# Gates of A and B, the first merge stage and branch A's merge products computed half of the tokens at a time

## What is computed

```python
def merge_and_residual(x, h, gate, br, a_out, b_out, c_out, lw):
    ya = (a_out.reshape(B, T, A_WIDTH) * jax.nn.silu(br['ga'])) @ lw['w_proj_a']
    yb = (b_out.reshape(B, T, B_WIDTH) * jax.nn.silu(br['gb'])) @ lw['w_proj_b']
    yc = (c_out * jax.nn.silu(br['gc'])) @ lw['w_proj_c']
    g_a, g_b, g_c = jnp.split(jax.nn.sigmoid(h @ lw['w_gate'] + lw['b_gate']), N_BRANCH, axis=-1)
    y = (g_a * ya + g_b * yb + g_c * yc) @ lw['w_out']
    return layer_norm(DEEPNORM_ALPHA * x + gate * y, lw['ln_g'], lw['ln_b'])
```

## Time and profile before

| what | value |
|---|---|
| median of 3 runs | 1398.67 us (1397.64 to 1399.9) |
| the profiled execution | 1399.68 us |
| span in its profile | 1397.9 us |
| PE busy | 1361.0 us, 97% of the span |
| ACT, DVE, POOL busy | 627.7, 769.3, 682.8 us |
| PE's waits for ACT at L987 (gates) | 1.6 us in 4 |
| PE's waits for DVE at L987 (y) | 1.9 us in 4 |
| PE's wait "issue" at L987 | 1.7 us, once |

### The profile page before, as it was taken

How to read it: one execution, slowest core, us unless ns; L and a number is a source line. 1 busy time by engine, 2 the same in 40 slices (tenths; PEclk the granted TensorE clock), 3 DMA queues, 4 the chain that set the end, 5 groups by cost and what they waited for, 6 DMA issues and landing times.

```text
span 1397.9 us, 22509 instructions
## 1 busy us (share of the span) xinstructions
PE 1361.0 (97%) x8654; PEld 1260.6 (90%) x8654; DVE 769.3 (55%) x1618; ACT 627.7 (45%) x1314; POOL 682.8 (49%) x490
## 2 busy tenths in 40 slices
PE   7999999999999999999999999999999999999997
PEld 5898989899899999999888988998989989999986
DVE  5756773163883511656695567732558725037558
ACT  5436876334765211213264468851367733122131
POOL 3455565234565354344654566643246554444450
PEclk9999999999999999999999999999999999999999
DMA  9312001122013254354321210011211041225321
GB/s 378 122 61 80 17 31 46 61 80 76 31 47 115 82 167 154 103 211 137 121 105 56 70 61 31 17 60 62 78 60 46 31 136 61 75 76 196 121 91 75
DMA packets 36761, 126.87 MB, mean 91 GB/s; under 512 B 5040, under 2 KB 5808, under 8 KB 36656
## 3 DMA queue, kind: packets, MB, share of 16 engines
q1 hardware_dynamic: 29952, 108.54, 22.9%
q10 hardware_dynamic: 6704, 16.90, 3.3%
HBM read 119.66 MB, written 5.77 MB: 90 GB/s over the span
## 4 chain that ended last, share of the span: by engine, by line
PE 88%; DVE 4%; POOL 2%; ACT 2%; issue 2%; DVEq 0%; ACTq 0%; POOLq 0%
PE ps L987 42%; PE ps L968 8%; PE ps L919 7%; PE ps L921 7%; PE ps L920 7%; PE ps L1137 4%; PE ps L1127 3%; PE ps L1129 3%; PE ps L1148 2%; PE ps L1149 2%; PE ps L1004 1%; POOL w_lo L1854 1%; POOL p_f_a L1880 1%; PE ps L1156 1%; PE ps L1012 1%
## 5 line engine op out<-in xcount | busy, mean ns | idle before, releaser
L1854 POOL TENSOR_TENSOR w_lo<-raw,w_hi 128x1024 fp32r<-128x1024 f32 x148 | 360.0, 2438 | 270.6 <-ACT w_hi L1192 185.0
L987 PE MATMUL ps<-h_hi,w_hi 128*128 128x320 f32 x992 | 230.0, 313 | 3.3 <-issue 1.7
L987 PE MATMUL ps<-h_hi,w_lo 128*128 128x320 f32 x992 | 227.2, 310 | 0.0
L987 PE MATMUL ps<-h_lo,w_hi 128*128 128x320 f32 x992 | 226.6, 310 | 0.0
L1192 ACT ACTIVATE w_hi<-raw 128x1024 fp32r<-128x1024 f32 x148 | 154.4, 1055 | 148.2 <-DMA raw<-in_weights 66.2
L987 PEld LDWEIGHTS ps<-h_hi,w_hi 128*128 128x128 f32 x992 | 170.0, 189 | 16.1 <-issue 3.9
L987 PEld LDWEIGHTS ps<-h_hi,w_lo 128*128 128x128 f32 x992 | 166.8, 189 | 0.0
L987 PEld LDWEIGHTS ps<-h_lo,w_hi 128*128 128x128 f32 x992 | 166.7, 189 | 0.0
L919 PE MATMUL ps<-w_hi,h_hi 128*128 128x512 f32 (+1 forms) x360 | 129.2, 359 | 1.2 <-POOL w_lo L1854 1.0
L921 PE MATMUL ps<-w_hi,h_lo 128*128 128x512 f32 (+1 forms) x360 | 127.6, 354 | 0.0
L920 PE MATMUL ps<-w_lo,h_hi 128*128 128x512 f32 (+1 forms) x360 | 127.5, 354 | 0.0
(11 more groups left out here) (194 smaller groups left out, 3044.8 us busy)
## 6 DMA issues: line engine op xcount, KB each, us to landing
raw<-in_weights SPq DMA_DIRECT2D x190, 512.0 KB, 3.3
raw_more<-in_weights SPq DMA_DIRECT2D x10, 512.0 KB, 10.4
x<-in_x_sample ACTq DMA_DIRECT2D x6, 512.0 KB, 9.6
x_mid<-x ACTq DMA_DIRECT2D x5, 512.0 KB, 2.6
x<-x_mid ACTq DMA_DIRECT2D x5, 512.0 KB, 7.1
y_sample<-x SPq DMA_DIRECT2D x3, 512.0 KB, 2.6
pack<-in_pack ACTq DMA_DIRECT2D x2, 528.0 KB, 6.5
x<-in_x_sample SPq DMA_DIRECT2D x2, 512.0 KB, 5.1
```

The source lines that it names most:

```text
L987: last = pe.matmul(ps[:, s + half, 0:HALF], w[:, u % RING, cols], acts[:, k, half * HALF:(half + 1) * HALF], start=k == 0 and part == 0, s ...
L1854: did(pool.tensor_tensor(w_lo[:, n % RING, :], raw_tile(r), w_hi[:, n % RING, :], ALU.subtract), w_ready)
```

## The change

Sixteen stages in each layer now go by halves: the four gates of A, the first three gates of B, the first merge stage of branch A (z 0) and the eight y of branch A. Their first halves get events of their own (`g1`, `z1`, `y1`), which `whole` puts in front of the stage's own event. Each half takes a single bank, by the rule for single banks; the stages that were by halves before stay pinned to 6 and 7 (`in_steps`). `half_rows` now also serves a whole stage in one piece: all matmuls of the first half, then all of the second, and PE waits for each bank when its half begins. ACT's Silu and copy and DVE's product are done once a half on 128x320 numbers. POOL's product of attention and gate waits for both halves of the gate; ACT's sigmoid of z 0 waits for both halves of z 0. Loads, splits and the order of all other events are as before.

```diff
--- before.py
+++ after.py
@@ -92,15 +92,20 @@
 
 def by_halves(stage):
 
+    return stage[0] == "gT" or stage[0] == "y" and stage[2] == 0 or stage[0] == "z" and stage[2:] == (0, 0)
+
+
+def in_steps(stage):
+
     return stage[0] == "gT" and (stage[2] in ("c", "u") or stage[2:] == ("b", KT_B - 1))
 
 
 def first_half(stage):
-    return ("g1", *stage[1:])
+    return (stage[0][0] + "1", *stage[1:])
 
 
 def whole(stage):
-    return chunks(stage, 1) + [stage]
+    return chunks(stage, 1) + ([first_half(stage)] if by_halves(stage) else []) + [stage]
 
 
 def attention(l, br, first_filler, filler, last_filler, lag, ahead):
@@ -546,9 +551,9 @@
             take(("out", e[1], 1, e[2]), 1, until=("out", e[1], 1, e[2]))
         elif kind == "cr" and by_halves(e[2]):
             if e[3] == 0:
-                take(first_half(e[2]), 1, 6, until=first_half(e[2]))
-            elif e[3] == GATE_CHUNKS // 2:
-                take(e[2], 1, 7, until=e[2])
+                take(first_half(e[2]), 1, 6 if in_steps(e[2]) else None, until=first_half(e[2]))
+            if e[3] == e[4] // 2:
+                take(e[2], 1, 7 if in_steps(e[2]) else None, until=e[2])
         elif kind == "cr" and e[3] == 0:
             take(e[2], 2, until=e[2])
         elif kind == "mm" and e[3] == 0:
@@ -955,31 +960,34 @@
                     if not ends:
                         did(last, w_used)
 
-                def half_rows(stage, i):
-                    half, u, each = 2 * i // GATE_CHUNKS, USERS[stage], KT_D * 3 // (GATE_CHUNKS // 2)
-                    mine = stage if half else first_half(stage)
-                    s, i = PLACE[mine][0], i % (GATE_CHUNKS // 2)
+                def rows_of(stage):
+                    if stage[0] == "y":
+                        return o_hi, o_lo, KT_B, stage[3] % 2 * KT_B * P
+                    return h_hi, h_lo, KT_D, 0
+
+                def half_rows(stage, i, n):
+                    u = USERS[stage]
                     if i == 0:
-                        begin(mine)
                         pe.wait_ge(w_ready, u + 1)
-                    work = [(k, part) for k in range(KT_D) for part in range(3)]
-                    for k, part in work[each * i:each * (i + 1)]:
-                        w, acts = ((w_hi, h_hi), (w_hi, h_lo), (w_lo, h_hi))[part]
-                        last = pe.matmul(ps[:, s, 0:HALF], w[:, u % RING, k * P:(k + 1) * P],
-                                         acts[:, k, half * HALF:(half + 1) * HALF],
-                                         start=k == 0 and part == 0, stop=k == KT_D - 1 and part == 2)
-                    if i == GATE_CHUNKS // 2 - 1:
-                        did(last, filled[s])
+                    hi, lo, kt, first = rows_of(stage)
+                    work = [(half, k, part) for half in range(2) for k in range(kt) for part in range(3)]
+                    for half, k, part in work[len(work) * i // n:len(work) * (i + 1) // n]:
+                        mine = stage if half else first_half(stage)
+                        s, opens, closes = PLACE[mine][0], (k, part) == (0, 0), (k, part) == (kt - 1, 2)
+                        if opens:
+                            begin(mine)
+                        w, acts = ((w_hi, hi), (w_hi, lo), (w_lo, hi))[part]
+                        last = pe.matmul(ps[:, s, 0:HALF], w[:, u % RING, first + k * P:first + (k + 1) * P],
+                                         acts[:, k, half * HALF:(half + 1) * HALF], start=opens, stop=closes)
+                        if closes:
+                            did(last, filled[s])
 
                 def channel_rows(stage, i, n):
                     s, u = PLACE[stage][0], USERS[stage]
                     if i == 0:
                         begin(stage)
                         pe.wait_ge(w_ready, u + 1)
-                    if stage[0] == "y":
-                        hi, lo, kt, first = o_hi, o_lo, KT_B, stage[3] % 2 * KT_B * P
-                    else:
-                        hi, lo, kt, first = h_hi, h_lo, KT_D, 0
+                    hi, lo, kt, first = rows_of(stage)
                     work = [(k, part, half) for k in range(kt) for part in range(3) for half in range(2)]
                     for k, part, half in work[len(work) * i // n:len(work) * (i + 1) // n]:
                         w, acts = ((w_hi, hi), (w_hi, lo), (w_lo, hi))[part]
@@ -1078,7 +1086,7 @@
                             else:
                                 pe.wait_ge(o_done, O_PER_LAYER * l + (10, 20)[stage[2]])
                         if by_halves(stage):
-                            half_rows(stage, i)
+                            half_rows(stage, i, n)
                         else:
                             channel_rows(stage, i, n)
                     elif kind == "kt":
@@ -1381,8 +1389,8 @@
                         if br == "u":
                             continue
                         s = wait_filled(act, e)
-                        if kind == "g1" or e in TANH_NO:
-                            half = (g_c if br == "c" else g_t)[:, c, HALF * (kind == "gT"):HALF * (1 + (kind == "gT"))]
+                        half = (g_c if br == "c" else g_t)[:, c, HALF * (kind == "gT"):HALF * (1 + (kind == "gT"))]
+                        if in_steps(("gT", *e[1:])):
                             did(act.activation(half, ps[:, s, 0:HALF], ACT.Copy, scale=0.5), drained[s])
                             if kind == "g1":
                                 continue
@@ -1397,8 +1405,10 @@
                             wait_filled(act, ("in", l, "kv_a", T - 1))
                         if br == "b" and c == 0:
                             wait_filled(act, ("y", l, 0, KT_D - 1))
-                        did(act.activation(g_t[:, c, :].rearrange("p (b n) -> p b n", b=2), ps[:, s:s + 2, 0:HALF], ACT.Silu),
-                            drained[s])
+                        did(act.activation(half, ps[:, s, 0:HALF], ACT.Silu), drained[s])
+                    elif kind in ("z1", "z") and e[2:] == (0, 0):
+                        s, first = wait_filled(act, e), HALF * (kind == "z")
+                        did(act.activation(merge[:, 0, first:first + HALF], ps[:, s, 0:HALF], ACT.Copy), drained[s])
                     elif kind == "z":
                         _, l, r, j = e
                         s = wait_filled(act, e)
@@ -1415,6 +1425,8 @@
                                                ACT.Sigmoid, bias=b_gate_col[:, r * KT_D + j:r * KT_D + j + 1]), drained[s])
                     elif kind == "sg":
                         _, l, j = e
+                        if j == 0:
+                            wait_drained(act, ("z1", l, 0, 0))
                         wait_drained(act, ("z", l, 0, j))
                         did(act.activation(merge[:, j, :], merge[:, j, :], ACT.Sigmoid, bias=b_gate_col[:, j:j + 1]), sg_ready)
                     elif kind == "mix":
@@ -1745,15 +1757,17 @@
                             dve.wait_ge(gate_made, TANH_NO[("gT", l, "c", KT_B - 1)] + 1)
                         half = g_c[:, c, HALF * (kind == "gT"):HALF * (1 + (kind == "gT"))]
                         did(dve.tensor_tensor(half, ps[:, s, 0:HALF], half, ALU.mult), drained[s])
+                    elif kind in ("y1", "y") and e[2] == 0:
+                        _, l, _, j = e
+                        s = wait_filled(dve, e)
+                        dve.wait_ge(sg_ready, KT_D * l + j + 1)
+                        half = merge[:, j, HALF * (kind == "y"):HALF * (1 + (kind == "y"))]
+                        did(dve.tensor_tensor(half, ps[:, s, 0:HALF], half, ALU.mult), drained[s])
                     elif kind == "y":
                         _, l, r, j = e
                         s = wait_filled(dve, e)
                         y = ps[:, s:s + 2, 0:HALF]
-                        if r == 0:
-                            dve.wait_ge(sg_ready, KT_D * l + j + 1)
-                            m2 = merge[:, j, :].rearrange("p (b n) -> p b n", b=2)
-                            did(dve.tensor_tensor(m2, y, m2, ALU.mult), drained[s])
-                        else:
+                        if r > 0:
                             wait_drained(dve, ("z", l, r, j))
                             n = 2 * KT_D * l + (r - 1) * KT_D + j
                             if n >= 2:
@@ -1887,6 +1901,7 @@
                         if gate in TANH_NO:
                             pool.wait_ge(gate_made, TANH_NO[gate] + 1)
                         else:
+                            wait_drained(pool, first_half(gate))
                             wait_drained(pool, gate)
                         did(pool.tensor_tensor(og_sum(n), og_sum(n), og_part(g_t, g), ALU.mult), og_ready)
                     elif kind == "ol":
```

## The result

The changed kernel takes 1388.43 us (1388.33 to 1388.55, 4 runs) against 1398.16 (1397.24 to 1399.9, 4 runs) for the one before: ratio 0.9929, 95% interval 0.9912 to 0.9946. That is 9.7 us less, inside the stated range and 0.07 us from the forecast.

The account below looks back on a forecast made before the run. PE bounds the kernel, so its idle time counts. Terms 1.47 + 1.46 + 5.8 + 1.46 = 10.19 us off the profiled 1399.68 gave 1389.5, less 1.01 for the median: 1388.5; range 1385.5 to 1394.0.

Parts of the forecast that it names:

- The eight waits: PE's four waits on gate drains and four on y products, both layers: all vanish, 5.53 us, each y 0.73.
- Layer 1's gates: Layer 1's start of A: two gate waits and the shorter last drain, 0.81 + 0.60 + 0.27 = 1.68 us.
- layer 0's gates: Layer 0's start of A: two gate waits and the shorter last drain, 2 x 0.60 + 0.27 = 1.47 us.
- The start of A in layer 1: Branch A's attention in layer 1: first and second maximum start sooner, 5.8 us, between 1.68 and 6.7.
- the wait at z 1: Layer 1: PE's 1.69 us "issue" was bank 7 holding tile 4's transposed queries; it goes.
- the half clock: Layer 1, 805.9 to 812.6: PE's 0.50 clock behind the idle stretches goes, saving up to 3.35 us.
- layer 0's clock: Layer 0, 119.8 to 123.1: the half-clock stretch stays; if it moved or went, 1.65 us either way.
- A: Rival: only the marked waits go, layer 1's wait or clock fall stays; gain 6.1, 1392.6 us; chance 0.20.
- C: Rival: in 32 stages, separating matmuls with shared weights costs time, about 1472 us; decides from 17.7 ns a pair; chance 0.05.
- B: Rival: new idle at attention starts makes the clock fall elsewhere, price 1.7 to 3.4 us, 1390 to 1392; chance 0.12.
- D: Rival: time doesn't move, same banks or gains lost at next waits; 1395.8 to 1399 us; chance 0.07.
- Gates B at 0: Shorter last drains of gates B and z: counted as 0, bound 0.27 us a layer.

Follow-up runs that it names:

- experiment 3: Kernel before with only the sixteen y of branch A by halves: 1396.63 us, ratio 0.9985.
- experiment 4: Changed kernel with the sixteen y of branch A whole again: 1391.29 us.
- experiment 1: Kernel before with only the eight gates of A by halves; gates of B, z and y whole: 1400.5 us, ratio 1.0015.
- experiment 6: Changed kernel with layer 1's transposed queries of tile 4 put in bank 7: 1391.39 us.
- 5: Kernel before, no halves, with layer 1's transposed queries of tile 4 in bank 0 instead of 7, tile 0's kept in bank 3: 1396.32 us, ratio 0.9983.
- 7: Changed kernel with the still whole stages running all first-half matmuls before the second half's, banks and drains unchanged: 1389.89 us.
- experiment 11: Changed kernel run again unaltered, on the chip of the follow-up runs: 1389.25 us.
- experiment 8: Changed kernel with the first three gates of B whole again: 1389.01 us.
- experiment 2: Kernel before with only gates of A by halves and layer 0's whole z 0 put in banks 1 and 2: 1397.27 us, ratio 0.9987.
- 10: Changed kernel with ACT's load of the exp table moved between the two drains of z 0 in both layers: 1387.05 us.

## Why the prediction was right, and where it was not

**The eight waits** went in full. The y were worth 2.98 by the leads of experiment 3 and 2.0 to 2.9 by the times of experiment 4, against 2.92. Layer 1's gates gave 1.81 with their shorter drain in experiment 1, against 1.68; layer 0's gates 1.52 against 1.47: the kernel after came to gate 1 0.31 us later (its transposes at 66.70 against 66.39, out of a start that the change doesn't touch) and led by 1.21 (110.84 - 109.63) when the keys' work began behind the last gate.

**The start of A in layer 1** gave 5.84, against 5.8. Its parts were not known singly, and the runs give them: 1.81 for the gates (experiment 1), 1.38 for the wait at z 1 (experiment 6), 2.75 for the half clock (experiment 3; its bound was 3.35). Together that is 5.94, close to the whole, though each part comes from another kernel. That the "issue" was a bank is shown from both sides (5 and 6).

**The step that failed** is layer 0's clock, "the keys' waits before it aren't touched", so the stretch "stays". The waits stayed and the stretch was gone: 1.4 us, from a lead of 1.21 to 2.63. PE's two waits for keys, before and after:

```profile
115.13 0.41 PE L1096 MATMUL ps<-ident_r,k_st 128*128 128x128 f32 x2 [1.08 <-DVE k_st L1521]
118.36 0.30 PE L1127 MATMUL ps<-k_hi,q_t 128*128 128x128 f32 x1 [1.40 <-DVE k_lo L1661]
```

```profile
113.92 0.41 PE L1104 MATMUL ps<-ident_r,k_st 128*128 128x128 f32 x2 [0.81 <-DVE k_st L1533]
117.15 0.30 PE L1135 MATMUL ps<-k_hi,q_t 128*128 128x128 f32 x1 [1.39 <-DVE k_lo L1673]
```

The first is 0.27 us shorter, as much as the last gate's drain; no run shows whether that decides. It is hardly chance alone: the stretch is there in all three profiles with whole gates of A (before, experiments 3 and 5), and in none of the nine profiles with halved gates besides experiment 1, whose half clock comes earlier, behind its 4.06 us. Why the clock stays up there with the halves is open. The range had it as 1.65 either way.

The other slip is the 1.01 us by which the profiled execution stood above the median: I took it off the forecast as if the changed kernel had it too. It does not: 1388.39 and 1388.43. The two errors, 1.1 too little and 1.0 too much, cancel in the median, so that it came within 0.07 us is luck; against the profile the forecast was 1389.5 and not 1388.4. One thing may be behind both. The fastest run of before, beside experiment 1, took 1396.21 us at a mean clock of 0.999; its runs around 1400 are at 0.995. Between the fastest runs of both the change is worth 1396.21 - 1388.33 = 7.9 us; the other two of the 9.7 would then be falls that before has in more of its executions than the changed kernel. That is read from mean clocks; only one execution of before was profiled.

**The rivals.** A fell in 5 and 6 and C in 7, as told there. B did not come in the two profiles of the changed kernel, which have no fall at a start of attention; its slower runs in experiment 11 were not profiled. D fell with the time and the waits view. None of them named what experiment 1 found: the gates of A by halves, made alone, make the kernel slower.

**Gates B at 0** was right (experiment 8). Layer 0's and layer 1's stretches with y and B gained 0.1 to 0.2 us more than the y term, which is too small for these runs to place.

## What to carry to other kernels

Where results rotate through few banks, look at who held a bank last and which engine drains it, not at how many banks there are: an "issue" wait of the matmul engine was a bank twice here, once for 1.7 and once for 4.06 us. In both cases the stage that waited needed two neighbouring banks, and when some stages are freed of that need the map changes for those that are left, so change them together and read the new map. A table load that stands in a chain belongs where its engine waits anyway; that gave 1.5 us in layer 0 and nothing in layer 1, where the next wait took its place.

## What was not expected of the hardware

The granted clock does not fall after every idle stretch of the same kind. A wait of 1.7 to 1.8 us at the same place was followed by 0.50 in the profile of before and by 1.00 in experiments 3 and 6; the slightly longer ones of experiments 1 and 2, 1.95 and 1.96 us, were followed by 0.50. A stretch at 0.50 came near 26 us in the profiles of experiments 6, 7 and 10 and in none of the others, though the kernels do not differ there; behind it these executions were 1.2 to 1.5 us later than the changed kernel. The window in experiment 6 and, with 1.00, in experiment 11:

```profile
24.50:29.00 4.50, 4.38 (x18) 3.64 (x19) 3.88 (x10) 3.10 (x6) 0.00 (x0) 0.69 1.01 401
```

```profile
24.50:28.00 3.50, 2.92 (x17) 2.59 (x18) 2.88 (x9) 2.11 (x6) 0.00 (x0) 1.00 0.86 302
```

One profile is one throw, and a forecast from it should say which falls it holds.

DVE's addition on the cached values (L1678) took 1.77 us at 114.69 in the changed kernel while POOL was splitting weights, and 0.27 in experiment 1, where POOL was idle. DVE and POOL, first in the changed kernel, then in experiment 1:

```profile
113.86 7.19 POOL L1868 TENSOR_TENSOR w_lo<-raw,w_hi 128x1024 fp32r<-128x1024 f32 x3 [0.61 <-DVE k_st L1533]
114.69 1.77 DVE L1678 TENSOR_TENSOR vv<-pack,vv 128x128 fp32r<-128x128 f32 x1
```

```profile
120.27 0.27 DVE L1682 TENSOR_TENSOR vv<-pack,vv 128x128 fp32r<-128x128 f32 x1
121.70 2.40 POOL L1876 TENSOR_TENSOR w_lo<-raw,w_hi 128x1024 fp32r<-128x1024 f32 x1 [5.66 <-ACT w_hi L1200]
```

PE's wait for the last keys behind it was 1.39 us in the one and 0.66 in the other. The Trainium skill ("SBUF — State Buffer", section "SBUF: two separate sides") has DVE and GpSimd share a pair of ports that one of them holds for a whole instruction while the other stands still; it says so of a DVE operation with two inputs in SBUF, as this addition is, beside a GpSimd operation that reads SBUF. These rows agree with it: the addition ends at 116.46, just behind the first of the three splits, which by a third of 7.19 us ends near 116.26. No run here moved POOL's split alone, so it isn't shown by an experiment.
